# Three transitions from an output projection over a norm to the next projections, by halves of the tokens, in a three-block transformer kernel

## The reference

```python
# first block, after its mixing
x = x + y @ w_out                                     # residual after mix 1
h = rms_norm(x, ffn_norm_g)                           # n2
u = h @ w_up                                          # first tiles of MLP 1

# between the second and the third block
h = h + y @ w_out_2                                   # residual after mix 2
h = rms_norm(h, final_g_2)                            # n5
h = layer_norm(h, ln_in_g_3, ln_in_b_3)               # l1
proj = h @ w_in_3                                     # k and v of the window, then the rest

# third block, after its mixing
h = layer_norm(ALPHA * h + mix, ln1_g_3, ln1_b_3)     # l2, mix = y @ w_out_3
gate, up = split(h @ w_gate_up_3)                     # first tiles of MLP 3
```

## Time and profile before

| | |
|---|---|
| median of 3 runs | 3109.94 us (3109.58 to 3111.23) |
| the profiled execution's own time | 3108.35 us |
| its span in the profile | 3106.7 us |
| mean granted TensorE clock | 0.978 of full speed |
| busy share PE, DVE, ACT | 94%, 61%, 41% |
| instructions | 35319 |
| DMA | 141.69 MB, mean 46 GB/s |

### The profile page before, as it was taken

The page is one execution under the profiler, slowest core; times in us unless marked ns, Lnnn a source line. Parts: engine busy times, 40 slices in busy tenths (PEclk is TensorE's granted clock), DMA queues, the critical chain, the costliest instruction groups (busy, mean ns, idle before and its releaser), DMA issues.

```text
span 3106.7 us, 35319 instructions
## 1 busy us (share of the span) xinstructions
PE 2933.6 (94%) x14242; PEld 2273.0 (73%) x14242; DVE 1899.1 (61%) x2790; ACT 1280.6 (41%) x1991; POOL 2.2 (0%) x6
## 2 busy tenths in 40 slices
PE   8999799999999998999998989999888999999997
PEld 6787587788888876777765757665566888888885
DVE  5543438777777776876673463667664755555556
ACT  4223415434434444445446253555543533233323
POOL 0000000000000000000000000000000000000000
PEclk9999899999999999999999999999989999999999
DMA  4211111111111111111110101000001111111111
GB/s 152 73 54 45 31 48 34 55 41 55 59 50 55 43 53 42 40 35 41 30 32 21 41 27 35 24 19 28 22 27 34 41 55 55 55 45 51 61 48 68
DMA packets 48831, 141.69 MB, mean 46 GB/s; under 512 B 12790, under 2 KB 16670, under 8 KB 48542
## 3 DMA queue, kind: packets, MB, share of 16 engines
q1 hardware_dynamic: 48670, 139.45, 14.4%
HBM read 135.16 MB, written 9.77 MB: 47 GB/s over the span
## 4 chain that ended last, share of the span: by engine, by line
PE 80%; DVE 8%; ACT 6%; issue 5%; DMA 0%; SPq 0%; DVEq 0%; ACTq 0%
PE psum L747 22%; PE psum L517 16%; PE psum L787 13%; PE psum L980 10%; PE psum L551 6%; PE psum L573 2%; PE psum L887 2%; PE psum L562 1%; PE psum L1062 1%; PE psum L1089 1%; PE psum L568 1%; PE psum L907 1%; PE psum L619 1%; DVE mlp_ta L2297 1%; DVE residual L2412 1%
## 5 line engine op out<-in xcount | busy, mean ns | idle before, releaser
L1999 ACT ACTIVATE w_hi<-w_raw 128x512 fp32r<-128x512 f32 x288 | 179.8, 625 | 316.8 <-DVE w_raw L2966 192.7
L2412 DVE TENSOR_TENSOR residual<-residual,psum 128x1024 f32<-128x1024 f32 x176 | 213.9, 1220 | 137.4 <-PE psum L787 137.3
L747 PE MATMUL psum<-h_hi,w_hi 128*128 128x512 f32 x640 | 249.0, 389 | 0.0
L747 PE MATMUL psum<-h_hi,w_lo 128*128 128x512 f32 x640 | 249.0, 389 | 0.0
L747 PE MATMUL psum<-h_lo,w_hi 128*128 128x512 f32 x640 | 248.9, 389 | 0.0
L517 PE MATMUL psum<-h_hi,w_hi 128*128 128x512 f32 x768 | 240.9, 395 | 7.3 <-DVE ret_q L2205 3.3
L517 PE MATMUL psum<-h_hi,w_lo 128*128 128x512 f32 x768 | 236.7, 389 | 0.0
L517 PE MATMUL psum<-h_lo,w_hi 128*128 128x512 f32 x768 | 236.7, 389 | 0.0
L787 PE MATMUL psum<-mlp_act_hi,w_hi 128*128 128x512 f32 x704 | 219.8, 393 | 13.8 <-DVE residual L2412 8.7
L2989 DVE TENSOR_TENSOR w_lo<-w_raw,w_hi 128x512 fp32r<-128x512 f32 x288 | 197.7, 687 | 38.3 <-ACT w_hi L1999 38.2
L787 PE MATMUL psum<-mlp_act_lo,w_hi 128*128 128x512 f32 x704 | 218.1, 391 | 0.0
(11 more groups left out here) (356 smaller groups left out, 5411.5 us busy)
## 6 DMA issues: line engine op xcount, KB each, us to landing
w_raw<-in_weights SPq DMA_DIRECT2D x228, 512.0 KB, 3.5
residual<-in_x_t SPq DMA_DIRECT2D x8, 512.0 KB, 9.7
out_t<-residual SPq DMA_DIRECT2D x8, 512.0 KB, 3.0
rel_copies<-rel_rows SPq DMA_DIRECT2D x8, 480.0 KB, 6.0
na_bias<-rel_copies SPq DMA_DIRECT2D x8, 240.0 KB, 4.5
band_copies<-band_rows SPq DMA_DIRECT2D x8, 192.0 KB, 6.1
ret_rotary<-in_rotary SPq DMA_DIRECT2D x1, 1024.0 KB, 12.4
swa_bias<-band_copies SPq DMA_DIRECT2D x4, 256.0 KB, 2.8
```

The costliest lines, as they stand in the source:

```text
L747: ins = self.pe.matmul(out[bank[j]], w[:, k, :], x(k), start=(j in emptied and k == 0 and part == 0), stop=(k == 3 and part == 2), skip_gr ...
L1999: self.act.activation(dst, m.block_source(plan, n), ACT.Copy).then_inc(*self.to("mw_hi_" + name, n))
L2412: self.dve.tensor_tensor(x, x, self.m.place["down", t, n], ALU.add).then_inc(*self.to("dve_down", t, n))
```

## The change

The last tile of each of the three output projections and the pair after it are done by halves of the tokens. `project_halves` computes the last tile for tokens 0 to 511 and then for 512 to 1023, and within the second half it issues the mean of the first. `project_pair_halves` computes both weight tiles for the first half of the tokens and then both for the second. Everything of the norm (residual, sums, centring, squares, root, scaling, high and low part) becomes two operations on 512 columns, with the order of the two halves written out anew on ACT and DVE. Only the keep stays at 1024 columns. The half means and half variances have PSUM banks of their own, taken one bank at a time (`take(..., bank, 1)`). In T2 and T3, the eight variance matmuls of the first half come ahead of the pair, those of the second are issued one by one within the pair's first half, by the table `steps` (after part k of the second weight tile). In T1 the mean of the second half is issued within it, after part 2 of the first tile. SP's queue is the same row by row.

The core of the diff (line numbers of `L5xx` to `L28xx` in the order rows of the change are those of the new file):

```diff
+    def project_halves(self, emptied, step):
...
+        for half, s in halves():
+            for k in range(KD):
+                if half and k == 4:
+                    step()
+                for part, (w, low) in enumerate(((w_hi, 0), (w_lo, 0), (w_hi, 1))):
+                    ins = self.pe.matmul(out[:, s], w[:, k, :], self.h(k, low)[:, s], start=(k == 0 and part == 0),
+                                         stop=(k == KD - 1 and part == 2))
+            ins.then_inc(*self.to("proj", t, *upto(half)))
+        self.tile += 1
+
+    def project_pair_halves(self, h_hi, h_lo, emptied0, emptied1, steps):
...
+        first = [(k, j) for j in range(2) for k in range(3)] + [(k, j) for k in range(3, KD) for j in range(2)]
+        second = [(k, j) for k in range(KD - 3) for j in range(2)] + [(k, j) for j in range(2) for k in range(KD - 3, KD)]
+        for half, s in halves():
+            for k, j in (first, second)[half]:
...
+                if not half and (k, j) in steps:
+                    steps[k, j]()
+        self.tile += 2
...
+    def half_variance(self, name, k, half, bank, bufs, *emptied):
+
+        told, s = f"pe_{name}_var", slice(half * HALF, half * HALF + HALF)
+        if k == 0:
+            self.take((told, half), bank, 1, *emptied)
+        self.q.wait_ge(*self.on(f"act_{name}_sq", k, half))
+        self.pe.matmul(self.m.place[told, half], self.m.c("mean1024"), bufs[k % 2][:, s], start=(k == 0), stop=(k == KD - 1),
+                       skip_group_check=True).then_inc(*self.to(told, k, half))
...
-        self.mix_out("1")
-        self.mean_after_mix("n2")
-        self.mlp(PLAN1, "n2")
+        self.mix_out("1", lambda: self.n2_mean(0))
+        self.mlp(PLAN1, "n2", {(2, 0): lambda: self.n2_mean(1)})
...
-        self.mix_out("3", lambda: self.window_mean())
-        self.means_after_mix3()
-        self.mlp(PLAN3, "l2")
+        self.mix_out("3", lambda: self.l2_mean(0), lambda: self.window_mean())
+        for k in range(KD):
+            self.l2_variance(k, 0)
+        self.l2_mean(1)
+        self.mlp(PLAN3, "l2", {(k, 1): lambda k=k: self.l2_variance(k, 1) for k in range(KD)})
...
+        rstd(0)
+        high(0, 0)
+        q.wait_ge(*on("dve_mix1", KD - 1))
+        self.half_square("n2", 1, KD - 1)
         self.split_up_to(MLP1 + 1)
-        self.rsqrt(m.place[("pe_n2_mean",)], m.n_rstd, EPS, ("pe_n2_mean",), ("act_n2_rstd",))
-        self.high_parts("n2", m.normed)
+        high(1, 0)
+        high(2, 0)
+        rstd(1)
+        for k in range(3, KD):
+            high(k, 0)
+        for k in range(KD):
+            high(k, 1)
...
+        for k in range(KD):
+            self.high_half("l1", k, 0, "ln_in_b_3")
+            self.centred_half("l1", k, 1, bufs)
+        rstd(1)
+        for k in range(KD + 1):
+            if k < KD:
+                self.high_half("l1", k, 1, "ln_in_b_3")
+            if k:
+                self.keep("l1", k - 1, 1.0, m.v("ln_in_b_3", k - 1))
+
+    def centred_half(self, name, k, half, bufs):
+
+        s = slice(half * HALF, half * HALF + HALF)
+        if k >= 2:
+            self.q.wait_ge(*self.on(f"pe_{name}_var", k - 2, half))
+        self.q.wait_ge(*self.on(f"dve_{name}_cent", k, half))
+        self.act.activation(bufs[k % 2][:, s], self.m.x[:, k, s], ACT.Square).then_inc(*self.to(f"act_{name}_sq", k, half))
...
+        last_tile(0)
+        for k in range(KD):
+            centre(k, 0)
+        first(0)
+        last_tile(1)
+        variance(0)
         self.split_up_to(B3 + 1)
...
+        centre(0, 1)
+        centre(1, 1)
+        rstd(0)
         for k in range(KD + 1):
             if k < KD:
+                self.scale_half("l1", k, 0, m.m_rstd, "ln_in_g_3")
             if k:
+                self.low_half("l1", k - 1, 0, "ln_in_b_3")
+            if k + 2 < KD:
+                centre(k + 2, 1)
+            if k == 3:
+                first(1)
+        variance(1)
+        rstd(1)
```

More of the change, by code:

```diff
@@ L460, in halves, with upto @@
     return [(h, slice(h * HALF, (h + 1) * HALF)) for h in range(2)]
+def upto(half):
+    return () if half else (0,)
 def key_row(r):
@@ new lines, in half_mean @@
+    def half_mean(self, told, half, bank, src, *emptied):
+        out = self.take((told, half), bank, 1, *emptied)
+        self.pe.matmul(out, self.m.c("mean1024"), src[:, half * HALF:half * HALF + HALF], start=True, stop=True).then_inc(
+            *self.to(told, half))
+    def half_variance(self, name, k, half, bank, bufs, *emptied):
[5 more added lines that the diff above has]
+                       skip_group_check=True).then_inc(*self.to(told, k, half))
@@ L679, in gating, with mix_out @@
             ins.then_inc(*to("pe_smix", g))
-    def mix_out(self, block, between=None, parts=tuple(range(KD))):
+    def mix_out(self, block, last, between=None, parts=tuple(range(KD))):
         add = "dve_mix" + block
@@ L1307, in after_mix1 @@
         self.split_up_to(B1 + 26)
-        for n in range(KD):
+        for n in range(KD - 1):
             if n >= 2:
@@ L1738, in after_mix2 @@
             self.squares("n5", n, m.x[:, n, :])
-        self.split_up_to(B3 + 1)
-        self.rsqrt(m.place[("pe_n5_mean",)], m.n_rstd, EPS, ("pe_n5_mean",), ("act_n5_rstd",))
-        self.centred_squares("l1", (m.m_buf0, m.m_buf1))
-        for half, s in halves():
-            q.wait_ge(*on("dve_l1_var", half))
-            act.activation(m.m_rstd[:, s], m.m_rstd[:, s], ACT.Ln, bias=m.c(f"eps{LN_EPS}", 1)).then_inc(*to("act_l1_ln", half))
-            q.wait_ge(*on("act_l1_ln", half))
-            act.activation(m.m_rstd[:, s], m.m_rstd[:, s], ACT.Exp, scale=-0.5).then_inc(*to("act_l1_rstd", half))
@@ new lines, in high_half, with keep @@
+    def high_half(self, name, k, half, bias):
+        m, s = self.m, slice(half * HALF, half * HALF + HALF)
+        self.q.wait_ge(*self.on(f"dve_{name}_scaled", k, half))
+        self.act.activation(m.h_hi[:, k, s], m.x[:, k, s], ACT.Identity, bias=m.v(bias, k)).then_inc(*self.to(f"act_{name}_hi", k, half))
+    def keep(self, name, k, scale, bias):
+        x = self.m.x[:, k, :]
+        self.q.wait_ge(*self.on(f"dve_{name}_lo", k, 1))
+        self.act.activation(x, x, ACT.Identity, scale=scale, bias=bias).then_inc(*self.to(f"act_{name}_keep", k))
@@ new lines, in after_mix2, with scale_half @@
+        variance(1)
+        rstd(1)
+        for k in range(KD + 1):
+            if k < KD:
+                self.scale_half("l1", k, 1, m.m_rstd, "ln_in_g_3")
+            if k:
+                self.low_half("l1", k - 1, 1, "ln_in_b_3")
+    def scale_half(self, name, k, half, rstd, gain):
+        m, s = self.m, slice(half * HALF, half * HALF + HALF)
+        x = m.x[:, k, s]
+        self.after(f"dve_{name}_cent", k, half)
+        self.dve.scalar_tensor_tensor(x, x, m.v(gain, k), rstd[:, s], ALU.mult, ALU.mult).then_inc(
+            *self.to(f"dve_{name}_scaled", k, half))
@@ L2829, in after_mix3 @@
         q.wait_ge(*on("act_l1_keep", KD - 1))
-        for n in range(KD):
+        t, last = B3 + 25, KD - 1
+        for n in range(last):
             if n >= 2:
```

291 lines of the change are left out of this document (216 added, 75 removed).

## The result

The changed kernel takes 3116.41 us (median of 17 runs, 3114.40 to 3118.03), the kernel before 3109.84 (17 runs). The ratio is 1.0021, with a 95% interval of 1.0014 to 1.0029, so the change costs 6.6 us, between 4.4 and 9.0. The profiled execution took 3117.42 us, with a span of 3116.1 and a mean granted clock of 0.975.

A forecast was written before the change was run, and what follows sets the result against it. PE's waits and half-speed clock at three transitions bound the kernel. Full-clock terms -3.2 (T1), +0.5 (T2), -1.4 (T3) plus 8.5 slow clock give +4.4 on 3109.94, so 3114.3 us; range 3104 to 3121.

The forecast's parts named there:

- the likeliest case alone: Whole kernel: the author's own forecast without the rivals, 3111 to 3118 us, given a chance of 0.47.
- Starts and gaps: Pairs start 1.8, 14.8 and 11.6 us after the last projection tile; middle gaps 4.5 in T2, 3.0 in T3.
- The second halves: T2 and T3 pairs: ACT needs 1.65 us per part, PE 1.36, so the half takes 13.7 instead of 10.9.
- I charge each of these five places with one short stretch: Three pair fronts and two middle gaps: 1.7 us of slow clock each, 8.5 in all, between 0 and 15.0.
- Low clock for more than about 4 us per place: Sign of being wrong: slow clock in the charged places lasting more than about 4 us each.
- Split by transition: With the clock, T1 -1.5, T2 +3.9, T3 +2.0 us; at full clock gains of 3.2 and 1.4, T2 losing 0.5.
- Later stages lean on PE or DVE, so a shift is kept to the end: Stages behind the transitions: they pass on any shift unchanged.
- Rival A: Five charged places: part-busy PE stays slow, charge 15.0 us, result +10.9, 3120.8; chance 0.27.
- Rival B: Five charged places: the clock holds, charge 0, result -4.1 us, 3105.8; chance 0.14.
- Rival C: T2 and T3 second halves: ACT does not pace them, both end 2.8 us earlier; with clock holding -9.7, 3100.2; chance 0.08.
- Rival D: Whole change: it does not do what it says; given no share of the chance.
- taken so that only a gap drops the clock: Fronts of T1 and T3 stay at full clock: clock charge 5.1 instead of 8.5 us, sum +1.0 instead of +4.4.

The follow-up runs named there:

- gap_filled: Changed kernel plus matmuls that nobody reads in the middle gaps of T2's and T3's pairs (18 and 12); 3116.75 us, ratio to before 1.0021.
- only_t1: Changed kernel with the second and third transitions put back to the code before, only the first by halves; 3108.45 us, ratio to before 0.9997.
- keeps_late: Changed kernel with four of eight keeps between the second half's high parts, four later, in T2 and T3; 3115.16 us, ratio to before 1.0018.
- only_t2: Changed kernel with the first and third transitions put back to the code before, only the second by halves; 3112.05 us, ratio to before 1.0007.
- lead_two: Changed kernel with squares and variances of the second half two parts earlier in T2 and T3; 3101.97 us, ratio to before 0.9976.
- filled_and_late: Changed kernel with both edits, unread matmuls in the two middle gaps and the keeps moved; 3113.23 us, ratio to before 1.0013.
- only_t3: Changed kernel with the first and second transitions put back to the code before, only the third by halves; 3114.09 us, ratio to before 1.0013.
- both_tiles_front: Changed kernel with both weight tiles of a part from the first part on in T2 and T3; 3108.43 us, ratio to before 0.9996.
- all_together: Changed kernel with lead_two, both_tiles_front, keeps_late, MLP 3's first DVE sum behind the weight split, k copies in two halves; 3094.53 us, ratio to before 0.9949.
- together_filled: all_together plus twelve matmuls that nobody reads, in two gaps of T2; 3092.42 us, ratio to before 0.9945.

## Why the prediction was right, point by point

The time, 3116.4 for a forecast of 3114.3, lies in the range, and in that of the likeliest case alone, 3111 to 3118. It is a hair beyond the 0.2% from which I counted it as slower. The mechanism was the one forecast: early starts of the pairs, given back in their fronts, in the middle gaps and in second halves paced by ACT. That the number came out so near is partly luck, as the points below say. Point by point, from E:

| step | predicted | measured |
|---|---|---|
| T1 pair starts | 1.8 | 1.95 |
| T1 nine matmuls done | 7.5 | 7.9 |
| T1 low part 3 | 10.5 | 11.7 |
| T1 split of the second tile | 28.2 | 29.5 |
| T2 pair starts | 14.8 | 15.05 |
| T2 nine matmuls | 5.5 | 5.7 |
| T2 first half ends | 36.1 | 38.3 |
| T2 middle gap | 4.5 | 4.53 |
| T2 second half | 13.7 | 14.2 |
| T2 tile behind | 58.0 | 60.8 |
| T3 pair starts | 11.6 | 11.8 |
| T3 first half ends | 32.8 | 34.4 |
| T3 middle gap | 3.0 | 3.04 |
| T3 second half | 13.7 | 14.2 |
| T3 tile behind | 50.7 | 52.6 |

The predicted column is at full clock, so the clock is part of what stands between the two.

- **Starts and gaps.** The chains through DVE, ACT and PE that end each gap came out within 0.3 us. Right.
- **The second halves.** "ACT has a high part and a whole keep per part" was right, and gap_filled shows it. So was its price: in T2 the high parts start at 1854.93, 1856.59 and 1858.25, 1.66 apart, for 1.65 forecast. The half is 0.5 longer all the same. Its last part starts 10.85 us after the first matmul, and that part with the last nine matmuls of the second tile takes 3.35 more. The forecast does not show how it got from 1.65 per part to 13.7, so which of the two it had too small stays open.
- **"I charge each of these five places with one short stretch".** This is the step that failed, though its sum did not. Against the lengths forecast for full clock the three fronts took about 1.3 (T1, of which the measured low part 3 has 1.2), 1.9 (T2) and 1.4 (T3) more. The two middle gaps cost nothing, though the slow stretch was there for 5 to 6 us, since ACT hid it (14.20 us with and without it). A sixth place, the tile behind T2's pair, was missing from my list: 3.76 us of wait for the copies, then 48 matmuls in 12.77 instead of 10.88, so 1.9. In all about 6.5 for 8.5. By E the transitions then come to -1.9, +4.9 and +0.8, and T1 loses another 1.2 up to the fixed point in MLP 1, which only_t1 and keeps_late, with the same T1, do not lose (there it stays at -1.8): 5.0, where I had 4.4. So the sum came out because errors of the steps cancel, and that is luck. "Low clock for more than about 4 us per place" was one of my own signs of being wrong. It came true in T2 and T3, with 5 to 9 us per place.
- **Split by transition.** I had -1.5, +3.9 and +2.0 with the clock. The chains say -0.7, +4.9 and +0.8, and for T1 alone -1.75.
- **"Later stages lean on PE or DVE, so a shift is kept to the end".** Wrong in a way I had not thought of. A shift is kept, but between the profiles the clock of untouched stretches differs too: +1.3 to +1.6 in MLP 1 and block 2, -1.5 to -1.7 in attention (the kernel before has 0.50 from 1967 to 1970.3 us, where the changed kernel at the same work has 1.00), +3.3 in the last norm. In the two pairs of profiles that is 3.2 us net. I had it at nothing. How much of it an average execution has is not shown.
- **Rival A, the slow clock stays.** Its rows came true, 1823.70 to 1829.70 wholly at 0.50, its price did not. Where PE was slow, DVE or ACT was mostly the later one. **Rival B** is refuted by the clock in the fronts, 0.50 and 0.60. **Rival C**: keeps_late took ACT's pace away, and in T2 only 0.7 of the 2.8 per half came, since B did not hold; with full clock as well, 2.0. **Rival D**: no.

The Trainium skill ("TensorE: Matmul & The Clock Gate", Part 1), taken so that only a gap drops the clock, would have left the fronts of T1 and T3 at full clock. Both ran at 1.2 GHz before their tenth matmul, T3's from its third on (0.60 over the stretch). T3's stands behind a gap of 2.29 us, so it could be either. T1's decides: its clock is 0.88 from 471.2 to 474.7 us and 0.50 from there to 478.2, and the longest idle time in it is 1.40 us. The measurement decides for part-busy being enough.

## What to carry to other kernels

Splitting a chain of engines in two halves wins the early start of the first half, here 16 us in T2 and in T3, and loses it if the second half's dependent step (here the last variance, and the root behind it) is issued as the last thing of the first: move it a few units ahead, so that independent work is left to cover it. Where two bounds lie side by side, a fix of one can show nothing in its stretch until the other is gone too. And follow a saving to the next point that later work hangs on: 1.3 us won in the second half of T2 were lost in the next tile. Compare untouched stretches of the two traces as well, since of the 9.4 us between the first two profiles 3.2 lay behind the first transition in places that nobody edited. One profile is one execution: look at where it lies among the timed runs.

## What was not expected of the hardware

The same gap, 2.45 us ahead of the same four matmuls, is followed by full clock in before, only_t1, only_t2, lead_two, keeps_late and filled_and_late, and by low clock in only_t3, the changed kernel, gap_filled, both_tiles_front, all_together and together_filled; 2.40 us ahead of the sums of squares split the kernels otherwise again. Each time it is 1.5 to 1.7 us. The middle gap of T3, 3.04 us, is followed by 0.50 in the changed kernel and by 1.00 in keeps_late. So the length of a gap alone does not say what the clock does behind it. A second profile of two of the kernels gave the same answer in the last norm, but in the changed kernel not at the end of MLP 1 and not in attention. The same page of the Trainium skill says that the slow matmuls at a kernel's start vary from run to run. The mean granted clock of the 17 runs of the changed kernel, 0.974 to 0.977, varies too. No run shows what fixes where the low stretches fall.
